# Forget-gate bound computed ahead on another layout, and orders and buffers moved, in the second block of a two-block fp32 kernel

## What is computed

```python
lb_all = jnp.cumsum(jax.nn.softmax(hgrn_lb_logits, axis=0), axis=0)   # logits (2, 8 heads, 128)
proj = rmsnorm(h, attn_norm_g) @ w_in                                 # 7168 columns and 16 narrow ones
log_f = jnp.log(lb + (1.0 - lb) * jax.nn.sigmoid(z))                  # HGRN2 forget gate
k = (1.0 - lb) * jax.nn.sigmoid(-z)
qkv = causal_conv_silu(concat([b_q, b_k, b_v]), conv_w)               # 4 taps, 2048 channels
gq, gk = l2norm(qkv[..., :512]), l2norm(qkv[..., 512:1024])
M = eye + where(strict, (k*beta) @ k.T * L, 0); u = solve(M, v*beta); w = solve(M, k*beta*exp(gc))
o_b = gated_rmsnorm(o_b, b_z); h = h + concat([o_a, o_b]) @ w_out
```

## Time and profile before

| what | value |
|---|---|
| median of 3 runs (lowest to highest) | 3365.92 us (3362.89 to 3366.36) |
| the profiled execution | 3370.62 us, its span 3368.1 us |
| PE / DVE / ACT / POOL busy | 98% / 61% / 43% / 15% of the span |
| chain that ended last: PE / DVE / ACT | 91% / 4% / 2% |
| weight chunk, issue to landing | 4.9 us (in-projection) |

### The profile page before, as it was taken

One profiled execution on the slowest core, in us unless ns is written; L12 is line 12 of the kernel. 1 busy time (PEld: TensorE's weight loads), 2 busy tenths in 40 slices (PEclk: granted clock), 3 DMA queues, 4 the chain that ended last, 5 costly groups with the idle time before them and its releaser, 6 DMA issues.

```text
span 3368.1 us, 48327 instructions
## 1 busy us (share of the span) xinstructions
PE 3288.0 (98%) x20054; PEld 2910.8 (86%) x20054; DVE 2061.0 (61%) x1864; ACT 1456.9 (43%) x1253; POOL 490.6 (15%) x417
## 2 busy tenths in 40 slices
PE   7999999999999979989999999999999999999998
PEld 6888899999888858877879999999999888888886
DVE  4455565555555566765455788899974555555554
ACT  5564453333333454443334434455543433333333
POOL 0001000000000002124500000888850000000000
PEclk9999999999999989999999999999999999999999
DMA  6444465555555443332236455666776665566563
GB/s 252 161 163 150 168 222 188 187 187 187 187 187 187 140 141 119 126 137 101 71 131 232 181 214 212 222 227 233 246 248 225 263 235 224 226 249 239 225 242 117
DMA packets 129332, 644.16 MB, mean 191 GB/s; under 512 B 12576, under 2 KB 45600, under 8 KB 59808
## 3 DMA queue, kind: packets, MB, share of 16 engines
q1 hardware_dynamic: 96016, 624.17, 51.2%
q10 hardware_dynamic: 33168, 17.83, 1.8%
HBM read 606.30 MB, written 35.65 MB: 191 GB/s over the span
## 4 chain that ended last, share of the span: by engine, by line
PE 91%; DVE 4%; ACT 2%; issue 1%; SPq 1%; DMA 1%; POOL 0%; DVEq 0%; ACTq 0%; POOLq 0%
PE pj L285 12%; PE pj L283 12%; PE pj L284 12%; PE pj L271 7%; PE pj L270 7%; PE pj L269 7%; PE pj L814 3%; PE pj L815 3%; PE pj L816 3%; PE pj L1610 3%; PE pj L1611 3%; PE pj L1612 3%; PE pm L271 2%; PE pt L271 2%; PE pt L269 2%; PE pm L269 2%
## 5 line engine op out<-in xcount | busy, mean ns | idle before, releaser
L251 ACT ACTIVATE hi<-raw 128x2048 fp32r<-128x2048 f32 x535 | 1024.4, 1916 | 1436.3 <-PE pj L285 675.6
L258 DVE TENSOR_TENSOR lo<-raw,hi 128x2048 fp32r<-128x2048 f32 x400 | 917.3, 2293 | 725.8 <-ACT hi L251 725.1
L283 PE MATMUL pj<-xh,hi 128*128 128x256 f32 x3328 | 930.0, 279 | 0.0
L285 PE MATMUL pj<-xh,lo 128*128 128x256 f32 x3328 | 929.4, 279 | 0.0
L284 PE MATMUL pj<-xl,hi 128*128 128x256 f32 x3328 | 929.0, 279 | 0.0
L283 PEld LDWEIGHTS pj<-xh,hi 128*128 128x128 f32 x3328 | 625.8, 188 | 0.6
L284 PEld LDWEIGHTS pj<-xl,hi 128*128 128x128 f32 x3328 | 625.4, 188 | 0.7
L285 PEld LDWEIGHTS pj<-xh,lo 128*128 128x128 f32 x3328 | 625.5, 188 | 0.0
L258 DVE TENSOR_TENSOR lo_in<-raw,hi 128x2048 fp32r<-128x2048 f32 x135 | 312.5, 2316 | 277.9 <-ACT hi L251 277.4
L2288 POOL TENSOR_SCALAR hotA<-cst,slotT 128x128 fp32r<-128x128 f32 x256 | 335.4, 1327 | 482.8 <-ACT slotT L2131 432.4
L1610 PE MATMUL pj<-hi,xh 128*128 128x512 f32 x576 | 239.4, 416 | 12.2 <-ACT proj L1679 7.9
(11 more groups left out here) (382 smaller groups left out, 4284.2 us busy)
## 6 DMA issues: line engine op xcount, KB each, us to landing
raw<-w_peer SPq DMA_DIRECT2D x256, 1024.0 KB, 6.0
raw<-w_mlp SPq DMA_DIRECT2D x128, 1024.0 KB, 4.9
raw<-w_in SPq DMA_DIRECT2D x104, 1024.0 KB, 4.9
raw<-w_out SPq DMA_DIRECT2D x32, 1024.0 KB, 4.9
raw<-w_q SPq DMA_DIRECT2D x16, 1024.0 KB, 4.9
act_scratch<-hidU SPq DMA_DIRECT2D x32, 512.0 KB, 3.0
gates_scratch<-stage ACTq DMA_DIRECT2D x8, 2048.0 KB, 17.3
hidV<-act_scratch SPq DMA_DIRECT2D x32, 512.0 KB, 3.7
```

The source lines that it names most:

```text
L251: nc.scalar.activation(hi[:, j, :], raw[:, j, :], ACT.Copy).then_inc(hi_ready, 1)
L258: nc.vector.tensor_tensor(low(q)[:, j, :], raw[:, j, :], hi[:, j, :].bitcast(F32), ALU.subtract).then_inc(lo_ready, 1)
L283: nc.tensor.matmul(o, hi[:, j, cols], xh[:, k0 + k, :], start=clears, stop=False, skip_group_check=True)
L285: mm = nc.tensor.matmul(o, lo[:, j, cols], xh[:, k0 + k, :], start=False, stop=end and b % 2 == 1, skip_group_check=True)
```

## The change

The bound is computed in block 1 from 16 new columns of small, with the 128 channels of a head on the partitions (tiles of 8 or 16 columns): bound_dve at k = 7 and 9, bound_act at k = 8 (Exp) and k = 10, where ACT writes the result to an HBM scratch, 4 bytes a piece. In block 2 lb is loaded from the scratch, and forget_dve waits for it; the two bound calls at k = 8 are gone. In block 1 the squares of x move behind make_hi and one step later. In block 2 the copy and the output of the narrow columns stand ahead of make_lo, and PE turns them back at quarter 3 instead of 1. The first tap moves from DVE to ACT, the squares for the l2 norm from DVE to POOL. dB has four buffers (the two new ones lie on dkq and dkbT), so that POOL waits for PE's product i-3 instead of i-1, and PE waits for the DVE update i-1 where i < 6. The squares of the state output are taken tile by tile, the first at k = 59, and the gated norm of B is a step earlier (k = 60 and 61 on DVE, its Sqrt on ACT at k = 60 instead of 61).

```diff
@@ -867,17 +871,18 @@
...
                     evacuate(k // 4 - 1, 1)
-                if k in (1, 2):
-                    squares_act(act, 0, k - 1, (s_x, 16))
-                if k == 3:
-                    root_act(act, 0)
-                    tail_act(act, 0, 8)
...
                     make_hi(act, (k + 2) // SLOTS, (k + 2) % SLOTS)
+                if k in (2, 3):
+                    squares_act(act, 0, k - 2, (s_x, 16))
+                if k == 3:
+                    tail_act(act, 0, 8)
+                if k == 4:
+                    root_act(act, 0)
@@ -887,6 +892,8 @@
...
                 att1_act(act, n, k)
+                if k in (K_LF + 1, K_LF + 3):
+                    bound_act(act, (k - K_LF) // 2)
@@ -903,9 +910,9 @@
                 o = k - K_IN1
                 if o > 0 and o % 2 == 0:
                     add(o - 1, 1)
-                if k == 3:
+                if k == 4:
                     var_dve(dve, 0)
-                if k == 4:
+                if k == 5:
                     rstd_dve(dve, 0)
                     tail_dve(dve, 0, 8)
                 if k >= 1:
@@ -919,6 +926,8 @@
...
                 att1_dve(dve, n, k)
+                if k in (K_LF, K_LF + 2):
+                    bound_dve(dve, n, (k - K_LF) // 2)
@@ -965,23 +974,25 @@
...
-        def bound_act(act):
-            act.wait_ge(lb_steps, 2)
-            nc.scalar.activation(lb_e, lb[:, :, :], ACT.Exp).then_inc(lb_steps, 1)
-            act.wait_ge(lb_steps, 5)
-
-        def bound_dve(dve, n):
-            dve.wait_ge(lbl_in, 16)
-            nc.vector.tensor_tensor(lb_e[:, 0, :], lb[:, 0, :], lb[:, 1, :], ALU.max).then_inc(lb_steps, 1)
-            dve.wait_ge(lb_steps, 1)
-            nc.vector.tensor_tensor(lb[:, :, :], lb[:, :, :], lb_e[:, 0:1, :].broadcast_to([P, 2, H * P]), ALU.subtract).then_inc(lb_steps, 1)
-            dve.wait_ge(lb_steps, 3)
-            link(dve, dve_link, n, nc.vector.tensor_tensor(lb_e[:, 1, :], lb_e[:, 1, :], lb_e[:, 0, :], ALU.add))
-            link(dve, dve_link, n, nc.vector.reciprocal(lb[:, 0, :], lb_e[:, 1, :]))
-            nc.vector.tensor_tensor(lb[:, 0, :], lb_e[:, 0, :], lb[:, 0, :], ALU.mult).then_inc(lb_steps, 1)
-            dve.wait_ge(lb_steps, 4)
-            nc.vector.tensor_scalar(lb[:, 1, :], lb[:, 0, :], -1.0, 1.0, ALU.mult, ALU.add).then_inc(lb_steps, 1)
-            dve.wait_ge(lb_steps, 5)
+        def bound_act(act, part):
+            if part == 0:
+                act.wait_ge(lb_steps, 1)
+                nc.scalar.activation(lbw[:, :, :], lbw[:, :, :], ACT.Exp).then_inc(lb_steps, 1)
+            else:
+                act.wait_ge(lb_steps, 3)
+                act.dma_start(lb_d.rearrange("o j (h p) -> p (o j) h", p=P), lbw[:, :, :], allow_slow_non_contiguous=True).then_inc(lb_out, 16)
+
+        def bound_dve(dve, n, part):
+            logits = small[:, S_LBL:S_LBL + 2 * H].rearrange("p (j h) -> p j h", j=2)
+            if part == 0:
+                link(dve, dve_link, n, nc.vector.tensor_tensor(lbm[:, :], logits[:, 0, :], logits[:, 1, :], ALU.max))
+                nc.vector.tensor_tensor(lbw[:, :, :], logits, lbm[:, :].unsqueeze(1).broadcast_to([P, 2, H]), ALU.subtract).then_inc(lb_steps, 1)
+            else:
+                dve.wait_ge(lb_steps, 2)
+                link(dve, dve_link, n, nc.vector.tensor_tensor(lbm[:, :], lbw[:, 0, :], lbw[:, 1, :], ALU.add))
+                link(dve, dve_link, n, nc.vector.reciprocal(lbm[:, :], lbm[:, :]))
+                link(dve, dve_link, n, nc.vector.tensor_tensor(lbw[:, 0, :], lbw[:, 0, :], lbm[:, :], ALU.mult))
+                nc.vector.tensor_scalar(lbw[:, 1, :], lbw[:, 0, :], -1.0, 1.0, ALU.mult, ALU.add).then_inc(lb_steps, 1)
@@ -1151,6 +1162,7 @@
...
             over = lambda i, x_: lb[:, i, hcols(x_)].unsqueeze(1).broadcast_to([P, TT, H * P // 2])
+            dve.wait_ge(lbl_in, 16)
@@ -1179,6 +1191,7 @@
...
         dB = [s(f"dB{i}", [P, 4, P]) for i in range(2)]
+        dB += [sb(f"dB{i + 2}", [P, 4, P], at=at_z + i * 4 * 4 * P) for i in range(2)]
@@ -1248,6 +1262,13 @@
...
         def conv_act(act, p):
+            for c in (2 * p, 2 * p + 1):
+                if c < 16:
+                    act.wait_ge(c_T, c + 1)
+                    if c >= 4:
+                        act.wait_ge(c_B, c - 3)
+                    nc.scalar.activation(cy[c % 4][:, :], conv_bank(c), ACT.Copy,
+                                         scale=small[:, S_CONV + 4 * c + 3:S_CONV + 4 * c + 4]).then_inc(c_first, 1)
@@ -1262,18 +1283,15 @@
...
             c0 = 2 * p
-            for j in range(4):
+            for j in range(1, 4):
...
                     y_, x_ = cy[c % 4], conv_bank(c)
-                    if j == 0:
-                        dve.wait_ge(c_T, c + 1)
-                        if c >= 4:
-                            dve.wait_ge(c_B, c - 3)
-                        nc.vector.tensor_scalar(y_[:, :], x_, w(c, 3), None, ALU.mult).then_inc(c_tap, 1)
+                    if j == 1:
+                        dve.wait_ge(c_first, c + 1)
                     else:
-                        dve.wait_ge(c_tap, 3 * c0 + (c - c0) + 2 * (j - 1) + 1)
-                        ins = nc.vector.scalar_tensor_tensor(y_[:, j:], x_[:, 0:256 - j], w(c, 3 - j), y_[:, j:], ALU.mult, ALU.add)
-                        ins.then_inc(c_tap if j < 3 else c_y, 1)
+                        dve.wait_ge(c_tap, 2 * c0 + 2 * (j - 2) + (c - c0) + 1)
+                    ins = nc.vector.scalar_tensor_tensor(y_[:, j:], x_[:, 0:256 - j], w(c, 3 - j), y_[:, j:], ALU.mult, ALU.add)
+                    ins.then_inc(c_tap if j < 3 else c_y, 1)
@@ -1315,9 +1333,7 @@
...
             if part == 0:
-                qk = proj2[:, :, B_Q:B_Q + 1024]
-                dve.wait_ge(c_out, 8)
-                link(dve, dve_link, n, nc.vector.tensor_tensor(dsq[:, :, :], qk, qk, ALU.mult))
+                dve.wait_ge(l_sq, 1)
@@ -1327,6 +1343,11 @@
...
                     nc.vector.tensor_tensor(x_, x_, dn[:, 2, t, :].unsqueeze(2).broadcast_to([P, H, P]), ALU.mult).then_inc(l_step, 1)
+
+        def squares_pool(pool):
+            qk = proj2[:, :, B_Q:B_Q + 1024]
+            pool.wait_ge(c_out, 8)
+            nc.gpsimd.tensor_tensor(dsq[:, :, :], qk, qk, ALU.mult).then_inc(l_sq, 1)
@@ -1360,14 +1381,17 @@
...
                 pool.wait_ge(d_N, m + 1)
-                if i >= 2:
-                    pool.wait_ge(d_PP, i - 1)
-                if 2 <= i < 6:
-                    pool.wait_ge(d_TU, i - 1)
-                nc.gpsimd.tensor_tensor(dB[i % 2][:, :, :], dN[:, 4 * m:4 * m + 4, :],
+                if i == 2:
+                    pool.wait_ge(d_S, 4)
+                if i >= 4:
+                    pool.wait_ge(d_PP, i - 3)
+                if 4 <= i < 8:
+                    pool.wait_ge(d_TU, i - 3)
+                nc.gpsimd.tensor_tensor(dB[i % 4][:, :, :], dN[:, 4 * m:4 * m + 4, :],
...
                     scaled((i - 8) // H, (i - 8) % H)
+            pool.wait_ge(d_B, 4 * NL)
@@ -1416,13 +1440,13 @@
...
                     for a in range(4):
-                        mm = nc.tensor.transpose(pj[0][:, i % 2, a * P:(a + 1) * P], dB[i % 2][:, a, :], ident)
+                        mm = nc.tensor.transpose(pj[0][:, i % 2, a * P:(a + 1) * P], dB[i % 4][:, a, :], ident)
                 else:
-                    pe.wait_ge(d_TU, i - 3)
+                    pe.wait_ge(d_TU, i - 1 if i < 6 else i - 3)
...
                     for a in range(4):
-                        mm = nc.tensor.matmul(pj[0][:, i % 2, a * P:(a + 1) * P], dB[i % 2][:, a, :], dT[:, 4 * m + a, :], start=True, stop=True)
+                        mm = nc.tensor.matmul(pj[0][:, i % 2, a * P:(a + 1) * P], dB[i % 4][:, a, :], dT[:, 4 * m + a, :], start=True, stop=True)
@@ -1566,6 +1590,12 @@
...
+        def state_squares_dve(dve, n, t):
+            dve.wait_ge(f_dve, 2 * t + 2)
+            o = proj2[:, t, A_F:A_F + H * P]
+            link(dve, dve_link, n, nc.vector.tensor_tensor(dsq[:, t, :], o, o, ALU.mult))
+            link(dve, dve_link, n, nc.vector.tensor_reduce(mss[:, t, H:2 * H], dsq[:, t, :].rearrange("p (h n) -> p h n", n=P), AX.X, ALU.add))
+
@@ -1574,10 +1604,7 @@
...
                 else:
-                    dve.wait_ge(f_dve, 4)
-                    o = proj2[:, :, A_F:A_F + H * P]
-                    link(dve, dve_link, n, nc.vector.tensor_tensor(dsq[:, :, :], o, o, ALU.mult))
-                    link(dve, dve_link, n, nc.vector.tensor_reduce(mss[:, :, hs], dsq[:, :, :].rearrange("p t (h n) -> p t h n", n=P), AX.X, ALU.add))
+                    state_squares_dve(dve, n, 1)
@@ -1621,7 +1648,7 @@
...
                     tail_pe(pe, 1, 16)
-                if k == K_GATE and quarter == 1:
+                if k == K_GATE and quarter == 3:
@@ -1693,14 +1720,13 @@
...
                     act.wait_ge(nm_sq, 8)
-                    act.dma_start(lb, lbl_d.broadcast_to([P, 2, H * P])).then_inc(lbl_in, 16)
+                    act.wait_ge(lb_out, 16)
```

(21 more changed lines are left out.)

13 lines of the change are left out of this document (8 added, 5 removed).

## The result

The changed kernel takes 3318.48 us (median of 4, 3318.14 to 3324.79) against 3366.14 for the kernel before: ratio 0.986, 95% interval 0.985 to 0.987. The span went from 3368.1 to 3316.7 us.

What follows compares the result with a forecast made beforehand. TensorE, busy 98% of the span, bounds the kernel, so only its gaps of about 42 us can be won. Terms sum to -25.3 us, from 3370.6 to 3345.3, or 3341 from the median; range 3332 to 3357.

Steps and rivals of the forecast that it cites:

- start, squares of x moved: Block 1: moving the squares of x frees the high part of chunk 3 but not chunk 4; -0.5 us.
- block 1, Exp and write: Block 1: Exp and table load lengthen the q and k wait, +1.5 us; the bound's write 0, at most +3.
- chunk 9: Block 2: tail_t is copied behind one low part, not the whole bound; the excess goes, slow clock included: -15.3 us.
- convolution, 33 to 42: Block 2 chunks 33 to 42: first taps to ACT and squares to POOL cut the excess; -8.5 us (-10 to -3).
- inverse, 48 and 49: Block 2 chunks 48 and 49: four dB buffers let POOL work ahead; -4.5 us (-6 to -2).
- state's norm, 60 to 64: Block 2 chunks 60 to 64: the changed order adds a wait in chunk 62; +2.0 us (0 to +4).
- slid to the forget gate: No-effect rival: tail_t's wait moves to the forget gate, 15.3 us come back at chunk 12; 3366 us, chance 0.03.
- The ring of the convolution: Engines' cycle of hi, lo, eight taps, two Silus in chunks 33 to 42: a turn falls from 7.70 to 6.9 us.
- Silu wait: TensorE's waits for the convolution's Silu, 8.0 us before; sign of being right: none before chunk 42.
- The norm's wait: State's norm: chunk 62 waits 3.6 us instead of 1.2; sign of being right: 2 to 4 us for resid.
- The two waits for dB: Inverse, chunks 48 and 49: the 2.8 us wait becomes about 1.1 for DVE's first update, the 1.8 goes.
- the 4-byte write: Slower rival: if a piece of the bound's write cost over 25 ns, 41 us lost; 3382 us, chance 0.03.

Runs made afterwards that it cites:

- the kernel before at its places: Kernel before with 160 unused bytes per partition ahead of the tail weights, so xh, xl and later tiles lie where the change puts them; 3336.02 us, ratio 0.990.
- the best kernel: Changed kernel with bound on 8 rows, norm in old order, xh, xl and coef at byte 64, cV at 128, other later tiles at 160; 3269.86 us, ratio 0.971.

## Why the prediction was wrong

The run with 96 unused bytes has the change's schedule at the old matmul rate, so it can be set against the kernel before stretch by stretch; differences are those of TensorE's start times at equal matmul number.

| step of the prediction | forecast | measured |
|---|---|---|
| start, squares of x moved | -0.5 | -1.3 |
| block 1, Exp and write | +1.5 and 0 (at most +3) | +10.4 |
| chunk 9 | -15.3 | -15.4 (21.33 to 5.93) |
| convolution, 33 to 42 | -8.5 | -9.0 (76.26 to 67.23) |
| inverse, 48 and 49 | -4.5 | -3.3 (25.83 to 22.57) |
| state's norm, 60 to 64 | +2.0 | +1.5 (36.39 to 37.87) |
| what stands in no term | 0 | -2.3 |
| sum, spans | -25.3 | -19.4 |

In block 1 the 10.4 are 7.3 for the write and 1.5 for the Exp (both as between the changed kernel and the kernel before at its places), and 1.6 for a slower clock (0.88 from 78 to 92 us, 1.00 in the changed kernel). The -2.3 are 1.1 in chunk 50 and 1.3 in chunks 51 to 59, where the prediction left the small waits for dU at 0. Taken the other way round, at the new places, the parts are 17.1 us of schedule (3333.8 to 3316.7) and 34.3 of addresses.

**Right.** Chunk 9 is clean, and chunk 12 still waits 6.6 and 1.9 us, so nothing slid to the forget gate. The ring of the convolution turns in 6.9 us: low parts start at 1409.60 and 1416.52. No Silu wait comes before chunk 42, and there it is 2.3, forecast 2.5. The squares on GpSimd took 4.45 us (from 1432.2), and the low part that meets them, at 1430.94, keeps its 2.29. They overlap by 1.0 us (1432.25 to 1433.23) and neither is longer for it, unlike the dB of the earlier trace rows. The Trainium skill's "GPSIMD Engine Reference" has 4497 ns in its table of cycle accounting (section "Elementwise — side-by-side cycle accounting"), and my estimate from the earlier trace rows was 5.0: the table was the better one. Its advice against GpSimd (section "Engine selection") is right in price and without effect in this place, since nobody waits. The norm's wait is in chunk 62 (3.6 us, as forecast), and the wait for xl behind the lift went from 3.0 to 2.5; the prediction's list of waits had left it out, its term had not. Q and k wait 2.5 us once the write is out of the way, forecast 2.1. The two waits for dB are gone, but 1.2 and 1.9 us for dT stand in their place, more than the 1.1 allowed. So the schedule's parts came out well but for two: the schedule at the old matmul rate, 3350.23 us, lies in the forecast range.

**Wrong, the write.** "0, at most +3" rested on "chunk 14 has over 10 us in hand". It has, up to its own products: before, it lands at 95.23 us, its parts are made by 100.7, and its products begin at 111.3. It came 9 us late, and nobody waited for these products. But each engine keeps its order, and VectorE's copy of q and k stands behind chunk 14's low part: of the 7.9 us that ScalarE stood, TensorE waited 4.7 for that copy, and behind the wait its clock was 0.50 from 109.2 to 116.0 us. The forecast had this order in view for the Exp and not for the write. The write cost 7.5 us (block 1 with the write moved away, against the changed kernel). The mechanism stood among the rivals as "the 4-byte write", but with a piece at over 20 ns as its condition; it took 11.8 us / 2048 = 5.8 ns a piece, near the 4.2 from the earlier trace rows, and hurt anyway.

**Wrong, the inverse.** The term of -4.5 for four buffers was too large. The row of the table says 3.3, but the kernel before had a slower clock there (0.93 against 1.00), and with only the buffers changed 0.9 us are left: the waits for dB pass on to the update dT.

**Wrong, the frame.** This is what took the time out of the range. TensorE "is busy 98% of the span: only its gaps can be won", and with it "the change can hardly win more than 1.3%". That takes the length of a clean chunk as fixed, and a change of it stands in no term. It wasn't: of 51.4 us of span, 19.4 are schedule and 32.0 are 96 bytes of address, and the best kernel wins 2.9% over before. Nothing in the trace of before alone shows that 116.7 ns could be 113.3, and the page's mean of a record doesn't either (279 ns before, 278 or 279 after): the rate is seen only from start to start, or in the count of a stretch. But the diff shows three allocations ahead of xh; I had read them as space only.

**Open.** Why an address matters at all. The rate is steady over long stretches, mostly in a few steps (226.7, 228.9, 232.4, 233.3; 113.3, 116.7, 117.8, 120), and depends on the tiles of a product, on the products before it, and on what comes in between; whether it is reads of two operands that meet, no run shows. Only 0, 64, 128, 160 and 192 were tried, with hi and lo always at 128.

## What to carry to other kernels

Where TensorE is busy all the time, look at the time from one matmul to the next at full clock against that of another build: if it differs without a wait, try unused bytes ahead of its operands, one group of tiles at a time, since each group (and each product run in between) has its own best place. Compare two schedules only at equal places, or a padding of 96 bytes passes for 32 us of scheduling. And a write of 8 KB in 4-byte pieces delayed the weight chunk issued next to it by some 9 us on ScalarE's queue, and chunks by 3 to 10 us on GpSimd's: give it rows. When a chunk comes late, look not only at its own products but at everything that stands behind it in the order of each engine.
